# Attention on one core: waits that another wait or the queue's order covers are left out, and the planner counts two-part maxima as longer

## The chip, the cores and the metric

The kernel runs on one core of a Trainium2 chip. The metric is the device time of one execution in microseconds (us). TensorE (PE) multiplies matrices, VectorE (DVE), ScalarE (ACT) and GpSimd (POOL) work on tiles, SyncE (SP) issues most of the DMAs. Each engine works through a queue of its own, in order, and engines wait for each other on semaphores.

## The reference

One decoder block on `x` of 2048 x 1024 in float32: a norm and an input projection; eight heads of forgetting attention (FoX) and four heads of differential attention, each of them causal over 2048 positions; an output projection, a norm and a residual; and an MLP of width 4096 with squared ReLU. Only the attention matters here:

```
forgetting:    s = q k^T * scale + c_i - c_j     masked, p = softmax(s),  o = p v
differential:  s = q k^T * scale - slope * dist  for two maps of one head
               a = softmax(s0) - lam * softmax(s1),  o = rmsnorm(a v) * (1 - lam_init)
```

## The kernel before

**Tiling.** A *block* is 512 queries of one head (a FoX head has its blocks in pairs, `s` 0 and 1; a differential block has both maps). It is cut into four tiles of 128 queries, `a` = 3 to 0. A tile's keys, up to 2048, are taken in *scores* of at most 1024 keys: a tile with more than 1024 keys has two parts. All scores go through two buffers in PSUM, `ps_s`.

**Steps.** For each score: `score` (PE, products into `ps_s`), `max` (DVE, the negated maximum over the keys, L1468; for a second part also a tiny reduction over the two parts' maxima, `top`, L1472, which first waits for the reduction before it), `corr` (ACT, a second part's correction factor, L1400), `exp` (ACT, L1420, with its row sums). `fix` (POOL, L1322) scales a first part by the correction. For a differential tile, `chain` (DVE, L1489 to L1497) makes the factors from the sums, and `mix` adds the second map to the first (on POOL, or on DVE, or with `scale` on ACT). Then each block's probabilities are turned in *turns* of 128 keys: `turn` (PE, four transposes, L1581, into a ring of three PSUM tiles, `ps_t`), `hi` (ACT, L1438, a rounded copy), `lo` (DVE, L1477, the rest of it), `pv` (PE, L1596 to L1601, into `ps_o`). A block ends with `o_half` or `o_sq` (ACT, L1447, L1453), `o_add` (DVE), `rows`, `var`, `o_var`, `o_pow`, `spread` (PE, L1625), `o_scale` (DVE, L1533) and `store` (SP).

**The order.** `attention_steps` gives every step an engine, a time for which it holds the engine, a time until its result is there, what it comes after, and an urgency. `Walk.order` plays these steps through (forwards, backwards, forwards again, always the most urgent of those that are ready) and writes out one list of 3800 steps. Every engine, SP with its loads and stores among them, takes its own steps out of this one list and in its order. So on an engine the list fixes what stands before what, and a wait on that engine's result vouches for all that it did before.

**Waits.** An instruction waits for its semaphores with `wait_ge` calls ahead of it. Where there is more than one, the compiled program has, besides the wait that the instruction itself carries, an instruction EVENT_SEMAPHORE on the engine's queue ahead of it; the profile shows it under the line of the last of the calls. `hi` waits for its turn (`x_ready`, L1435) and for the `pv` that last read its buffer, four turns ago (`p_used`, L1437). `exp` waits for the turn that last read its place in `probs` (L1410), for the sums' former user (L1406, L1408), for its maximum (`maxed`, L1412), and in the second map for the `mix` two tiles back (L1248, called at L1419). `o_half` waits also on L1446, `o_sq` on L1452, `fix` on L1321, `chain` on L1487, `o_scale` on L1532.

Of the kernel before, what the change touches and what calls it, by code (L numbers as in the profile page):

```python
# [24 lines left out]
FOX, DIFF = 0, 1  # L25
# [768 lines left out]
PRING = 4  # L794
TRING = 3
SETS = 6
# [169 lines left out]
def attention_steps(blocks, scores, turns):  # L966
# [63 lines left out]
    for b in blocks:  # L1030
        ahead, mine, fox = by_block[b.n], turns_of[b.n], b.kind == FOX
        load("load_q", q_blocks[b.qb], b.n - 2, [("score", last_q[b.qb - 2])] if b.qb >= 2 else ())
        for k, sc in enumerate(ahead):
            at = b.n - 1 + SPREAD * k / len(ahead) - LEAD - (EARLY if not fox and b.J == 3 else 0)
            parts, two, keys = parts_of[b.n, sc.a, sc.s], sc.parts == 2, sc.lo + sc.width
            for p in pieces_of(sc):
                load_piece("load_k", b.u, p, b.n - 2)
            walk.step("score", sc, "PE", 0.0009 * sc.width + (0.06 if sc.part == sc.parts - 1 else 0), at + RUSH["score"],
                      [("exp", scores[sc.g - 2]) if sc.g >= 2 else None, ("load_q", q_blocks[b.qb])]
                      + [("load_k", (b.u, p)) for p in pieces_of(sc)], 0.0009 * sc.width + 0.22)  # L1040
            walk.step("max", sc, "DVE", 0.07 + 0.00104 * sc.width + (0.08 if sc.part else 0), at + RUSH["max"],
                      [("score", sc)], 0.14 + 0.00104 * sc.width + (0.14 if sc.part else 0))
            if sc.part:
                walk.step("corr", sc, "ACT", 0.19, at + RUSH["corr"], [("max", sc)], 0.29)
            after = [("max", sc)]
            if (fox or sc.s == 0) and former[b.n, sc.a] is not None:
                after.append(("turn", turns_of[former[b.n, sc.a]][-1]))
            if b.n >= SETS:
                after.append(("rows", blocks[b.n - SETS]))
            if not fox and sc.s == 1:  # L1050
                if sc.part == 0:
                    tiles.append((b.n, sc.a))
                after.append(("mix", tiles[-3]) if len(tiles) > 2 else None)
            walk.step("exp", sc, "ACT", 0.24 + 0.00084 * sc.width, at + RUSH["exp"], after, 0.34 + 0.00084 * sc.width)
            if sc.part and (fox or sc.s == 0):
                walk.step("fix", (b.n, sc.a), "POOL", 1.87, at + RUSH["fix"], [("corr", sc), ("exp", parts[0])])
            if not fox and sc.s == 1 and sc.part == sc.parts - 1:
                walk.step("chain", (b.n, sc.a), "DVE", 1.12 if two else 0.5, at + RUSH["chain"],
                          [("exp", sc), ("corr", sc) if two else None])
                if scaled(b, sc.a):  # L1060
                    walk.step("scale", (b.n, sc.a), "ACT", 0.3 + 0.00084 * keys, at + RUSH["mix"], [("chain", (b.n, sc.a))])
                    holder = "POOL", 0.15 + 0.0023 * keys
                elif on_vector(b, sc.a):
                    holder = "DVE", 1.5 if two else 0.1 + 0.0012 * keys
                else:
                    holder = "POOL", (0.8 if two else 0.4) + 0.0043 * keys
                walk.step("mix", (b.n, sc.a), *holder, at + RUSH["mix"],
                          [("scale" if scaled(b, sc.a) else "chain", (b.n, sc.a)), ("fix", (b.n, sc.a)) if two else None])
# [91 lines left out]
def attend(nc, ctx, keep, qk, vals, q_rows, k_rows, mixT, w_out, x):  # L1160
# [3 lines left out]
    turns = attention_turns(blocks)  # L1164
    opening = opening_tiles(scores)
    steps = [step for step in attention_steps(blocks, scores, turns) if step[1] not in opening]
    places, former = probability_columns(blocks)
    pairs = [[b for b in blocks if b.qb == q] for q in range(blocks[-1].qb + 1)]
    fetches, last_pair = fetched(blocks, scores)
# [5 lines left out]
    for what, arg in steps:  # L1175
        if what in ("turn", "var", "spread"):
            ring_at[what, arg] = ring
            ring += 1
    last_turn = {t.b: t for t in turns}
    last_score = {sc.b: sc for sc in scores}  # L1180
    top_no = {sc.g: n for n, sc in enumerate(sc for sc in scores if sc.part == 1)}
    fix_no = {at: n + 1 for n, at in enumerate((sc.b, sc.a) for sc in scores
# [3 lines left out]
    for sc in scores:  # L1186
        if blocks[sc.b].kind == DIFF and sc.s == 1 and sc.part == sc.parts - 1:
# [6 lines left out]
            chain_done[sc.b, sc.a] = chains  # L1194
            mix_done[sc.b, sc.a] = mixes[on_dve]
    tile_of = {n: at for at, n in tile_no.items()}

    def k_value(u, p, fox, diff):

# [47 lines left out]
    def wait_mixed(eng, b, a):  # L1247
        eng.wait_ge(mixed_dve if on_vector(blocks[b], a) else mixed, mix_done[b, a])  # L1248
# [58 lines left out]
    def gpsimd(pool):  # L1307
# [7 lines left out]
        for what, arg in steps:  # L1315
            if what == "fix":
                n, a = arg
                low = probs[:, places[n, a]:places[n, a] + 1024]
                first, second = (sc for sc in scores if (sc.b, sc.a) == arg and side(sc) == 0)
                pool.wait_ge(corrected, top_no[second.g] + 1)  # L1320
                pool.wait_ge(exped, first.g + 1)  # L1321
                pool.tensor_tensor(low, low, corr[:, n % SETS, a, 0:1].to_broadcast([P, 1024]), ALU.mult)\  # L1322
                    .then_inc(fixed, 1)
            elif what == "mix" and scaled(blocks[arg[0]], arg[1]):
# [69 lines left out]
    def scalar(act, then):  # L1394
        first_hi = next(arg for what, arg in steps if what == "hi")
        for what, arg in steps:
# [5 lines left out]
            elif what == "exp":  # L1402
                sc, par, s = arg, arg.b % SETS, side(arg)
                if sc.a == 3 and sc.part == 0 and s == 0 and sc.b >= SETS:
                    if blocks[sc.b - SETS].kind == FOX:
                        act.wait_ge(summed, fox_no[sc.b - SETS] + 1)  # L1406
                    else:
                        act.wait_ge(squared, diff_no[sc.b - SETS] + 1)  # L1408
                if sc.part == 0 and s == 0 and former[sc.b, sc.a] is not None:
                    act.wait_ge(x_ready, ring_at["turn", last_turn[former[sc.b, sc.a]]] + 1)  # L1410
                if sc.part == 0:
                    act.wait_ge(maxed, sc.g + 1)  # L1412
                    bias = nmax[:, par, sc.a, s, 0:1]
                else:
                    act.wait_ge(topped, top_no[sc.g] + 1)
                    bias = top[:, par, sc.a, s:s + 1]
                out = tile(sc) if s == 0 else tile1(sc)
                if s == 1 and sc.part == 0 and tile_no[sc.b, sc.a] >= 2:
                    wait_mixed(act, *tile_of[tile_no[sc.b, sc.a] - 2])  # L1419
                act.activation(out, ps_s[:, sc.g % 2, 0:sc.width], ACT.Exp, bias=bias,  # L1420
                               accum_out=rsum[:, par, sc.a, s, sc.part:sc.part + 1]).then_inc(exped, 1)
            elif what == "scale":
                (n, a), par, low = arg, arg[0] % SETS, 1024
                keys = (4 * blocks[n].J + a + 1) * P
                one = probs1[:, tile_no[arg] % 2, :]
                act.wait_ge(chained, chain_done[arg])
                act.activation(one[:, low:keys], one[:, low:keys], ACT.Copy,
                               scale=factor[:, par, a, 0:1]).then_inc(multiplied, 1)
                act.activation(one[:, 0:low], one[:, 0:low], ACT.Copy,
                               scale=factor[:, par, a, 1:2]).then_inc(multiplied, 1)  # L1430
            elif what == "hi":
                t, at = arg, ring_at["turn", arg]
                if t is first_hi:
                    wait_projected(act)
                act.wait_ge(x_ready, at + 1)  # L1435
                if t.n >= PRING:
                    act.wait_ge(p_used, t.n - PRING + 1)  # L1437
                act.activation(p_hi[:, t.n % PRING, t.off:512], ps_t[:, at % TRING, t.off:512], ACT.Copy)\  # L1438
                   .then_inc(hi_ready, 1)
                if t is last_turned:  # L1440
                    then()
            elif what == "o_half":
                f = fox_no[arg.n]
                act.wait_ge(p_used, last_turn[arg.n].n + 1)
                if arg.n:
                    act.wait_ge(o_free, arg.n)  # L1446
                act.activation(o_half[:, :], ps_o[64:P, :], ACT.Copy).then_inc(o_half_ready, 1)  # L1447
            elif what == "o_sq":
                d = diff_no[arg.n]
                act.wait_ge(p_used, last_turn[arg.n].n + 1)  # L1450
                if d:
                    act.wait_ge(x_ready, ring_at["var", diffs[d - 1]] + 1)  # L1452
                act.activation(o_sq[:, :], ps_o[:, :], ACT.Square).then_inc(o_squared, 1)  # L1453

    def vector(dve, then, between):
# [8 lines left out]
        for what, arg in steps:  # L1464
# [16 lines left out]
            elif what == "chain":  # L1481
                (n, a), par = arg, arg[0] % SETS
                last = max((sc for sc in scores if (sc.b, sc.a) == arg), key=lambda sc: sc.g)
                dve.wait_ge(exped, last.g + 1)
                sums = rsum[:, par, a, :, 0]
                if last.parts == 2:
                    dve.wait_ge(corrected, top_no[last.g] + 1)  # L1487
                    sums = total[:, par, a, :]
                    link(dve.tensor_scalar(sums[:, 0:1], rsum[:, par, a, 0, 0:1], corr[:, par, a, 0:1],  # L1489
                                           rsum[:, par, a, 0, 1:2], ALU.mult, ALU.add), False)  # L1490
# [36 lines left out]
            elif what == "o_scale":  # L1527
# [1 line left out]
                if q == last_spread:  # L1529
                    between()  # L1530
                dve.wait_ge(x_ready, at + 1)
                dve.wait_ge(o_free, pairs[q][-1].n + 1)  # L1532
                dve.tensor_tensor(o_sb[:, q % ORING, :], ps_t[:, at % TRING, :], o_sb[:, q % ORING, :], ALU.mult)\  # L1533
                   .then_inc(x_free, 1)
            elif what == "o_var":
# [1462 lines left out]
```

## Time and profile before

| what | value |
|---|---|
| time, median of 3 runs | 2789.02 us (2787.31 to 2791.25) |
| the profiled execution's own time | 2791.69 us |
| its span, first to last instruction | 2789.9 us |
| mean granted clock of TensorE | 0.995 |
| PE, DVE, ACT, POOL busy | 98%, 63%, 48%, 23% of the span |
| attention's own stretch | about 583 to 1370 us of the span |

The profile gives busy time by engine, by line and by stretch, the idle time of an engine ahead of an instruction with what ended it, and the chain of work that ended last. Ends of matmuls are modelled. An EVENT_SEMAPHORE is not counted as busy. `PEld` is PE's weight load, ACTq and the like are queues' own instructions.

### The profile page before, as it was taken

What the parts mean: (1) busy time and instruction counts of PE and PEld (TensorE: products, weight loads), DVE (VectorE), ACT (ScalarE), POOL (GpSimd) and SP (SyncE); (2) the same over time, 40 slices, a digit from 0 to 9 for tenths busy, and PEclk for the clock granted to TensorE, in tenths of its full rate; (3) what the DMA queues carried; (4) which work ended last, traced back from release to release, by engine and by line L of the source; (5) the groups of instructions that cost most, each with busy time, mean ns of one, the idle gap of its engine ahead of it and who ended that gap; (6) DMA issues with size and microseconds to landing.
All of it is one profiled execution on the core that took longest, in us unless ns stands there. A gap on an engine that the chain in (4) does not pass through costs nothing.

```text
span 2789.9 us, 36811 instructions
## 1 busy us (share of the span) xinstructions
PE 2726.0 (98%) x13362; PEld 2258.5 (81%) x13362; DVE 1751.8 (63%) x2495; ACT 1342.1 (48%) x2413; POOL 628.2 (23%) x558
## 2 busy tenths in 40 slices
PE   8999999989999999999999999999999999999998
PEld 6888888878788887887788788888888888888887
DVE  6211111169889899899746877887777545435567
ACT  5111111158789789688523544554444333322233
POOL 5220011125746656557311100000000000000012
PEclk9999999999999999999999999999999999999999
DMA  5343333464434515423347755575445566556666
GB/s 191 121 159 106 106 135 108 136 159 101 101 88 104 126 47 131 112 62 99 106 135 234 257 205 191 179 250 191 142 140 194 181 198 207 182 161 218 208 215 240
DMA packets 287660, 434.49 MB, mean 156 GB/s; under 512 B 19648, under 2 KB 134592, under 8 KB 287488
## 3 DMA queue, kind: packets, MB, share of 16 engines
q1 hardware_dynamic: 241664, 368.41, 42.5%
q10 hardware_dynamic: 45056, 63.05, 6.3%
q8 instruction: 101, 1.65, 0.2%
q0 software_dynamic: 768, 0.79, 0.1%
q14 instruction: 71, 0.58, 0.1%
HBM read 280.27 MB, written 151.91 MB: 155 GB/s over the span
## 4 chain that ended last, share of the span: by engine, by line
PE 85%; DVE 6%; issue 4%; ACT 2%; DMA 1%; POOL 0%; SPq 0%; POOLq 0%; ACTq 0%; DVEq 0%
PE ml_ps L2940 7%; PE ml_ps L2939 7%; PE ml_ps L2938 7%; PE ml_ps L2908 7%; PE ml_ps L2911 7%; PE ml_ps L2910 7%; PE at_ps_t L1581 5%; PE at_ps_s L1152 4%; PE pj_acc L769 4%; PE pj_acc L770 4%; PE pj_acc L771 4%; PE at_ps_s L1146 4%; DVE at_nmax L1468 2%; PE at_ps_o L1596 2%; PE at_ps_o L1597 2%
## 5 line engine op out<-in xcount | busy, mean ns | idle before, releaser
L1468 DVE TENSOR_REDUCE at_nmax<-at_ps_s 128x1 f32<-128x1024 f32 (+4 forms) x372 | 338.0, 915 | 32.6 <-PE at_ps_s L1152 30.7
L2908 PE MATMUL ml_ps<-ml_h_hiM,ml_w_hi 128*128 128x512 f32 x896 | 349.0, 389 | 1.1 <-DVE ml_t L2730 1.0
L2910 PE MATMUL ml_ps<-ml_h_loM,ml_w_hi 128*128 128x512 f32 x896 | 348.6, 389 | 0.0
L2911 PE MATMUL ml_ps<-ml_h_hiM,ml_w_lo 128*128 128x512 f32 x896 | 348.6, 389 | 0.0
L2938 PE MATMUL ml_ps<-ml_b_hi,ml_a_hi 128*128 128x512 f32 x896 | 348.5, 389 | 0.0
L2939 PE MATMUL ml_ps<-ml_b_lo,ml_a_hi 128*128 128x512 f32 x896 | 348.5, 389 | 0.0
L2940 PE MATMUL ml_ps<-ml_b_hi,ml_a_lo 128*128 128x512 f32 x896 | 348.5, 389 | 0.0
L651 DVE SCALAR_TENSOR_TENSOR pj_out_sb<-pj_acc,pj_out_sb 128x512 fp32r<-128x512 f32 x96 | 66.4, 692 | 413.6 <-ACT pj_out_sb L578 413.6
L1477 DVE TENSOR_TENSOR at_p_lo<-at_ps_t,at_p_hi 128x512 fp32r<-128x512 f32 x480 | 279.3, 604 | 33.9 <-ACT at_p_hi L1438 31.5
L1438 ACT ACTIVATE at_p_hi<-at_ps_t 128x512 fp32r<-128x512 f32 x480 | 248.0, 536 | 82.7 <-PE at_ps_t L1581 46.0
L2585 POOL TENSOR_SCALAR ml_ss<-ml_ss 128x1 f32<-128x1 f32 x16 | 17.6, 1099 | 1183.4 <-ACT ml_junk L2678 1183.1
L1581 PE MATMUL at_ps_t<-at_ident_r,at_probs 128*128 128x128 f32 x1632 | 251.8, 277 | 15.5 <-DVE at_p_lo L1477 10.2
L1420 ACT ACTIVATE at_probs<-at_ps_s,at_nmax 128x1024 f32<-128x1024 f32 (+3 forms) x244 | 230.0, 943 | 44.8 <-DVE at_nmax L1468 42.3
L578 ACT ACTIVATE pj_out_sb<-pj_acc 128x512 fp32r<-128x512 f32 x96 | 57.4, 598 | 402.6 <-PE pj_acc L771 268.9
L1581 PEld LDWEIGHTS at_ps_t<-at_ident_r,at_probs 128*128 128x128 f32 x1632 | 194.6, 142 | 58.4 <-DVE at_p_lo L1477 22.6
L1146 PE MATMUL at_ps_s<-at_k,at_q 128*128 128x512 f32 (+3 forms) x640 | 209.7, 393 | 17.8 <-ACT at_probs L1420 15.3
L1322 POOL TENSOR_TENSOR at_probs<-at_probs,at_corr 128x1024 f32<-128x1024 f32 x96 | 182.1, 1897 | 146.3 <-ACT at_corr L1400 146.0
L2365 ACT ACTIVATE ml_b_hi<-ml_b_raw 128x1024 fp32r<-128x1024 f32 x56 | 59.4, 1061 | 306.7 <-issue 159.4
L1152 PE MATMUL at_ps_s<-at_k,at_q 128*128 128x512 f32 (+3 forms) x640 | 203.1, 382 | 0.0
L2908 PEld LDWEIGHTS ml_ps<-ml_h_hiM,ml_w_hi 128*128 128x128 f32 x896 | 168.2, 188 | 36.7 <-issue 1.3
L2911 PEld LDWEIGHTS ml_ps<-ml_h_hiM,ml_w_lo 128*128 128x128 f32 x896 | 168.2, 188 | 35.0
L2939 PEld LDWEIGHTS ml_ps<-ml_b_lo,ml_a_hi 128*128 128x128 f32 x896 | 168.2, 188 | 35.0
(267 smaller groups left out, 5915.7 us busy)
## 6 DMA issues: line engine op xcount, KB each, us to landing
ml_a_raw<-ua SPq DMA_DIRECT2D x112, 512.0 KB, 3.8
qk<-pj_out_sb ACTq DMA_DIRECT2D x64, 512.0 KB, 2.8
ml_w_raw<-in_w_up_dram SPq DMA_DIRECT2D x64, 512.0 KB, 4.9
ua<-ml_t SPq DMA_DIRECT2D x128, 256.0 KB, 2.6
ml_b_raw<-in_w_down_dram SPq DMA_DIRECT2D x56, 512.0 KB, 4.8
at_q<-qk SPq DMA_DIRECT2D x96, 256.0 KB
at_k<-qk SPq DMA_DIRECT2D x96, 256.0 KB
ua<-ml_x SPq DMA_DIRECT2D x96, 256.0 KB, 2.5
```

The lines of the kernel that those rows point to most:

```text
L1146: pe.matmul(keep.ps_s[:, sc.g % 2, at:at + width], keep.q2[:, n, sc.s, q], keep.k2[:, slot, sc.s, 0:width], start=True, stop=False)
L1152: last = pe.matmul(keep.ps_s[:, sc.g % 2, at:at + width], keep.q1[:, n, sc.s, q], keep.k1[:, slot, sc.s, 0:width], start=False, stop=True)
L1438: act.activation(p_hi[:, t.n % PRING, t.off:512], ps_t[:, at % TRING, t.off:512], ACT.Copy)\
L1468: dve.tensor_reduce(nmax[:, par, sc.a, s, sc.part:sc.part + 1], ps_s[:, sc.g % 2, 0:sc.width], AX.X, ALU.max, negate=True).then_inc(maxed, 1)
L1477: dve.tensor_tensor(p_lo[:, t.n % PRING, t.off:512], ps_t[:, at % TRING, t.off:512], f32(p_hi[:, t.n % PRING, t.off:512]), ALU.subtract).t ...
L1581: last = pe.transpose(ps_t[:, at % TRING, a * P:(a + 1) * P], probs[:, key:key + P], ident)
L2908: pe.matmul(to, hi, h_hi[m][:, k, :], start=begins and k == 0, stop=False, skip_group_check=not begins)
L2910: pe.matmul(to, hi, h_lo[m][:, k, :], start=False, stop=False, skip_group_check=not begins)
L2911: last = pe.matmul(to, lo, h_hi[m][:, k, :], start=False, stop=k == 3, skip_group_check=not begins)
L2938: pe.matmul(to, hi, b_hi[b % 4][:, k, :], start=begin, stop=False)
L2939: pe.matmul(to, hi, b_lo[b % 4][:, k, :], start=False, stop=False)
L2940: last = pe.matmul(to, lo, b_hi[b % 4][:, k, :], start=False, stop=end)
```

## The change

There are two parts. In the planner the `max` of a second part holds DVE for 0.19 us more than its width asks for, where it was 0.08, and its result comes after 0.19 more, where it was 0.14. `Walk` and the urgencies stay as they are, so the list of steps may come out in another order, for all engines.

In the engines' programs a helper `precedes` tells which of two steps stands first in the list. A wait is left out where another one, or the order on the engine that is waited for, already makes sure of it: `hi` keeps one of its two waits, `exp` its maximum's and, if not vouched for, the others, `fix` and `chain` one of two, `o_half` one, `o_sq` and `o_scale` mostly one. What is computed stays the same, and so do all the instructions that compute.

```diff
-            walk.step("max", sc, "DVE", 0.07 + 0.00104 * sc.width + (0.08 if sc.part else 0), at + RUSH["max"],
-                      [("score", sc)], 0.14 + 0.00104 * sc.width + (0.14 if sc.part else 0))
+            walk.step("max", sc, "DVE", 0.07 + 0.00104 * sc.width + (0.19 if sc.part else 0), at + RUSH["max"],
+                      [("score", sc)], 0.14 + 0.00104 * sc.width + (0.19 if sc.part else 0))
...
+    place = {step: n for n, step in enumerate(steps)}
...
+    def precedes(one, other):
+        return place.get(one, -1) < place[other]
...
                 first, second = (sc for sc in scores if (sc.b, sc.a) == arg and side(sc) == 0)
-                pool.wait_ge(corrected, top_no[second.g] + 1)
-                pool.wait_ge(exped, first.g + 1)
+                if precedes(("exp", first), ("corr", second)):
+                    pool.wait_ge(corrected, top_no[second.g] + 1)
+                else:
+                    pool.wait_ge(exped, first.g + 1)
...
                 if sc.a == 3 and sc.part == 0 and s == 0 and sc.b >= SETS:
-                    if blocks[sc.b - SETS].kind == FOX:
-                        act.wait_ge(summed, fox_no[sc.b - SETS] + 1)
-                    else:
-                        act.wait_ge(squared, diff_no[sc.b - SETS] + 1)
+                    before = blocks[sc.b - SETS]
+                    if before.kind == FOX and not precedes(("spread", before.qb), ("score", sc)):
+                        act.wait_ge(summed, fox_no[before.n] + 1)
+                    if before.kind == DIFF and not precedes(("o_var", before), ("max", sc)):
+                        act.wait_ge(squared, diff_no[before.n] + 1)
                 if sc.part == 0 and s == 0 and former[sc.b, sc.a] is not None:
-                    act.wait_ge(x_ready, ring_at["turn", last_turn[former[sc.b, sc.a]]] + 1)
+                    turn = last_turn[former[sc.b, sc.a]]
+                    if not precedes(("turn", turn), ("score", sc)):
+                        act.wait_ge(x_ready, ring_at["turn", turn] + 1)
...
                 if s == 1 and sc.part == 0 and tile_no[sc.b, sc.a] >= 2:
-                    wait_mixed(act, *tile_of[tile_no[sc.b, sc.a] - 2])
+                    n, a = tile_of[tile_no[sc.b, sc.a] - 2]
+                    if not on_vector(blocks[n], a) or not precedes(("mix", (n, a)), ("max", sc)):
+                        wait_mixed(act, n, a)
...
-                act.wait_ge(x_ready, at + 1)
-                if t.n >= PRING:
+                if t.n >= PRING and precedes(("turn", t), ("pv", turns[t.n - PRING])):
                     act.wait_ge(p_used, t.n - PRING + 1)
+                else:
+                    act.wait_ge(x_ready, at + 1)
...
                 act.wait_ge(p_used, last_turn[arg.n].n + 1)
-                if arg.n:
-                    act.wait_ge(o_free, arg.n)
...
-                if d:
+                if d and not precedes(("var", diffs[d - 1]), ("pv", last_turn[arg.n])):
                     act.wait_ge(x_ready, ring_at["var", diffs[d - 1]] + 1)
...
-                dve.wait_ge(exped, last.g + 1)
                 sums = rsum[:, par, a, :, 0]
+                if last.parts == 1 or precedes(("corr", last), ("exp", last)):
+                    dve.wait_ge(exped, last.g + 1)
+                else:
+                    dve.wait_ge(corrected, top_no[last.g] + 1)
                 if last.parts == 2:
-                    dve.wait_ge(corrected, top_no[last.g] + 1)
...
-                dve.wait_ge(o_free, pairs[q][-1].n + 1)
+                follower = first_turn.get(pairs[q][-1].n + 1)
+                if follower is None or not precedes(("pv", follower), ("spread", q)):
+                    dve.wait_ge(o_free, pairs[q][-1].n + 1)
```

## Rows read from the trace of the kernel before

**Rows 1.** Busy time by stretch: us, busy (instructions) of each engine, clock, DMA.
```profile
583.00:1370.00 787.00, 753.26 (x4501) 629.25 (x4502) 707.25 (x1319) 646.59 (x1438) 457.02 (x350) 0.99 0.41 102
700.00:800.00 100.00, 94.15 (x566) 78.89 (x566) 86.52 (x176) 76.69 (x180) 60.06 (x47) 0.98 0.48 120
800.00:900.00 100.00, 97.54 (x584) 81.17 (x583) 94.17 (x162) 88.56 (x190) 57.03 (x43) 1.00 0.32 78
```

**Rows 2.** Chain that ended last in attention's stretch: by line.
```profile
by line: PE at_ps_t L1581 17.9%; PE at_ps_s L1152 13.1%; PE at_ps_s L1146 12.9%; DVE at_nmax L1468 7.5%; PE at_ps_o L1596 6.7%; PE at_ps_o L1597 6.6%; DVE at_p_lo L1477 4.9%; issue 4.7%; ACT at_probs L1420 4.0%; PE at_ps_o L1599 2.9%; PE at
```

**Rows 3.** What PE waited for in that stretch: us in total, times, longest.
```profile
PE at_ps_s L1146 <- ACT at_probs L1420: 15.3, 27, 1.0
PE at_ps_t L1581 <- DVE at_p_lo L1477: 10.2, 16, 3.4
PE at_ps_t L1608 <- DVE at_p_lo L1477: 3.5, 5, 1.1
```

**Rows 4.** What ACT, DVE and POOL waited for there, in the same columns.
```profile
ACT at_p_hi L1438 <- PE at_ps_t L1581: 46.0, 76, 2.1
ACT at_probs L1420 <- DVE at_nmax L1468: 42.3, 77, 1.5
ACT at_p_hi L1438 <- PE at_ps_o L1601: 15.7, 21, 1.4
ACT at_p_hi L1438 <- PE at_ps_o L1597: 12.1, 28, 4.2
...
DVE at_total L1489 <- ACT at_corr L1400: 2.1, 4, 0.5
...
POOL at_probs L1322 <- ACT at_corr L1400: 146.0, 74, 4.2
```

**Rows 5.** EVENT_SEMAPHORE by line: count, ns min/median/max, first and last start in us.
```profile
L1437 ACTq EVENT_SEMAPHORE  x476: 17/17/17, 589.4 to 1361.6; - x159
L1412 ACTq EVENT_SEMAPHORE  x170: 17/17/38, 622.5 to 1351.1; - x170
L1446 ACTq EVENT_SEMAPHORE  x31: 17/17/17, 595.8 to 1295.6; - x31
L1452 ACTq EVENT_SEMAPHORE  x15: 17/17/17, 751.9 to 1363.4; - x15
L1321 POOLq EVENT_SEMAPHORE  x96: 17/17/17, 599.4 to 1333.1; - x96
L1487 DVEq EVENT_SEMAPHORE  x32: 21/21/21, 691.8 to 1338.2; - x32
L1532 DVEq EVENT_SEMAPHORE  x32: 21/21/21, 599.3 to 1367.0; - x32
```

**Rows 6.** Timeline of DVE and ACT: start us, us, instruction, idle time before it.
```profile
854.51 0.95 DVE L1468 TENSOR_REDUCE at_nmax<-at_ps_s 128x1 f32<-128x768 f32 x1
...
855.49 0.15 DVE L1472 TENSOR_REDUCE at_top<-at_nmax 128x1 f32<-128x2 f32 x1
855.56 1.28 DVE L1477 TENSOR_TENSOR at_p_lo<-at_ps_t,at_p_hi 128x512 fp32r<-128x512 f32 x2
855.68 0.90 ACT L1420 ACTIVATE at_probs<-at_ps_s,at_top 128x768 f32<-128x768 f32 x1 [0.39 <-DVE at_top L1472]
...
856.57 0.97 ACT L1438 ACTIVATE at_p_hi<-at_ps_t 128x512 fp32r<-128x512 f32 x2
...
856.76 1.22 DVE L1468 TENSOR_REDUCE at_nmax<-at_ps_s 128x1 f32<-128x1024 f32 x1
...
857.42 0.30 ACT L1400 ACTIVATE at_corr<-at_nmax,at_top 128x1 f32<-128x1 f32 x1
...
857.89 0.68 DVE L1477 TENSOR_TENSOR at_p_lo<-at_ps_t,at_p_hi 128x512 fp32r<-128x512 f32 x1
...
858.07 1.12 ACT L1420 ACTIVATE at_probs<-at_ps_s,at_nmax 128x1024 f32<-128x1024 f32 x1 [0.34 <-DVE at_nmax L1468]
...
866.17 0.60 ACT L1438 ACTIVATE at_p_hi<-at_ps_t 128x512 fp32r<-128x512 f32 x1 [0.30 <-PE at_ps_o L1597]
...
866.66 1.01 ACT L1420 ACTIVATE at_probs<-at_ps_s,at_nmax 128x896 f32<-128x896 f32 x1
```

**Rows 7.** Group of the two-part maxima's second reduction in attention: busy us, mean ns.
```profile
L1472 DVE TENSOR_REDUCE at_top<-at_nmax 128x1 f32<-128x2 f32 x128 | 19.9, 155 | 4.4
```

More of the change, by code:

```diff
@@ L1178, in attend @@
             ring += 1
-    last_turn = {t.b: t for t in turns}
+    last_turn, first_turn = {t.b: t for t in turns}, {t.b: t for t in reversed(turns)}
     last_score = {sc.b: sc for sc in scores}
```

## The prediction

> **What bounds the kernel now.** I read busy time by stretch first. The change touches attention alone, 787 us of the span, and there PE is busy for 753.3 of them [rows 1], so PE idles for 33.7 us. That is all that better waits or a better order could win, since no matmul goes away. DVE is close behind with 707.3 us and ACT has 646.6. The stretches are not alike: from 800 to 900 us PE idles 2.46 us with DVE busy for 94.2, from 700 to 800 it idles 5.85 with DVE busy for 86.5 [rows 1]. Next, the chain that ended last. PE's lines lead it, but some 17% of it runs over DVE's maxima (7.5%), `lo` (4.9%) and ACT's `exp` (4.0%), with 4.7% of issue besides [rows 2]: that is where PE waits for someone. Third, whom PE waits for. Scores wait for the `exp` that frees their PSUM buffer, 15.3 us in 27 waits; turns and `var` wait for the `lo` that frees theirs, 13.7 us in 21 [rows 3]. The reader is to see that these are late answers from DVE's and ACT's queues. Whether an answer is late for its own latency or for what stands ahead of it in the queue decides what each part of the change can be worth.
>
> **Part one: the waits.** Each surplus wait is an EVENT_SEMAPHORE on its queue: 476 in front of `hi`, 170 in front of `exp`, 31 of `o_half`, 15 of `o_sq`, 96 of `fix`, 32 of `chain`, 32 of `o_scale` [rows 5]. I listed the kernel's present order and looked up both sides of each condition of the diff in it: 476 go at `hi` (309 times the turn's wait stays, 167 times the `pv`'s), 165 of 170 at `exp`, the first users' waits with them, 11 of the waits for a `mix`, all at `o_half`, `o_sq`, `fix` and `chain`, 15 of 32 at `o_scale`. That is some 840 instructions, nearly 700 of them on ACT.
>
> What is one worth? It depends on whether its engine is idle. Busy: the `exp` at 866.66 has a second wait and starts 0.11 us before the `hi` ahead of it ends (866.17 + 0.60); the `corr` at 857.42, which has one wait, starts 0.12 before the end of what is ahead of it (856.57 + 0.97) [rows 6]. So behind a busy engine the instruction costs nothing: the engine's own work hides it, and that cover goes only where the engine stands idle. Idle: the `exp` at 855.68 carries its only wait itself and starts 0.04 us after `top` ends (855.49 + 0.15); the one at 858.07 has its maximum's wait in the EVENT_SEMAPHORE and starts 0.09 after the reduction ends (856.76 + 1.22) [rows 6]. The late wait in the separate instruction costs 0.05 us.
>
> The Trainium skill's "VectorE: DVE Perf Modes", The DRAIN you can't avoid, says that a semaphore between two operations of a queue costs nothing extra; by it this whole part would be 0. The row with the busy engine agrees with it, the idle pair (0.09 against 0.04) does not.
>
> How often is the separate wait the late one? At most in all 77 waits of `exp` for a maximum, and in the 21 + 28 waits of `hi` for a `pv` [rows 4]; where a `hi` waits for its turn (76 times), that wait is the one that it carries itself, and nothing is won. So ACT's answers come earlier by at most 77 x 0.05 + 49 x 0.05 = 6.3 us in sum. PE feels that only where its own wait goes back to such an answer. The chain runs for about a quarter of its length over engines other than PE (the 17% named, issue, and smaller pieces) [rows 2], so I take a quarter: 1.6 us. The ends are 0 and 6.3. On POOL the `fix` idles for 146.0 us, always until `corr` [rows 4]; that wait stays, and the one dropped, for an `exp` that ACT did earlier, had long been met: 0. `chain` keeps the late one, 4 waits x 0.05 = 0.2, inside the 1.6. `o_half`, `o_sq` and `o_scale`: 0. No wait is added, so nothing new stands at the head of a queue.
>
> **Part two: the order.** What does a two-part maximum really hold? From the reduction's start at 854.51 to the next operation's at 855.56 are 1.05 us [rows 6]. The planner had 0.07 + 0.00104 x 768 + 0.08 = 0.95, and has 1.06 now. A one-part maximum of 1024 held 1.13 (856.76 to 857.89) [rows 6], as its formula says (1.135). So the new duration is the true one, and the plan before left out 0.11 us at each of 128 [rows 7], 14.1 us of DVE in all. In tiles with two parts DVE is nearly full (94.2 of 100), and there a plan that takes DVE for freer than it is puts `lo` and `max` later than PE needs them. That speaks for a gain. Against it: the list is made by picking the most urgent ready step with weights that stay as they are, and one longer step shifts picks on all five queues, loads and stores on SP among them, at places that have nothing to do with it; and the stretches with most idle time have DVE at 86.5, so that they lack no DVE time [rows 1]. No instruction is added or lost by this part, and every DMA is issued as before, a few steps sooner or later; PE's longest waits are for `exp` and `lo`, not for loads [rows 3].
>
> Bounds from the rows: were the whole of attention as good as 800 to 900, it would idle 787 x 2.46% = 19.4 us, 14.3 fewer; were it as bad as 700 to 800, 787 x 5.85% = 46.0, 12.3 more. Neither end is near: a reshuffle of one duration in a plan whose other durations already fit leaves most of the pattern. I take a tenth of the better end, 1.4 us of gain, because the duration is right now and nothing else is known of it.
>
> **The sum.** In the profiled execution's own time: 2791.69 - 1.6 - 1.4 = 2788.7. That execution stands 2.67 above the median of the runs, so for the median 2789.02 - 3.0 = 2786.0. What a measurement of this kernel can tell from no change is about 0.2%, 5.6 us: 2783.4 to 2794.6.
>
> **The rivals.**
>
> *The order wins several us.* PE's 15.3 and 13.7 us of waits are a lateness of DVE's and ACT's queues, and a plan with DVE's true load repairs them where it is fullest. If it takes a third of those 29.0, that is 9.7, with the 1.6 of the waits 11.3: 2777.7; with a fifth, 5.8 + 1.6: 2781.6. I put this case at 2780. For it: the 14.1 us missing from the plan. Against: the poor stretches are the ones with DVE free.
>
> *The order loses: slower than before.* The weights were fitted to a plan with the old duration. In the new plan DVE's maxima look more expensive, `lo` gets picked before `max` or the other way round at other places, and scores wait longer for `exp`. Its place is the score waits (15.3 us in 27). If they rise by 0.4 us each for twice as many, 27 x 0.4 = 10.8 less 1.6 of the waits: 2798; if by half of that, 2793, which counts as the same. It decides from an order that costs 7.2 us (5.6 + 1.6). For it: 12.3 us up to the worse stretch's level. Against: the new duration agrees with the timeline.
>
> *The waits do nothing.* Every late answer that PE feels comes from a queue that is busy ahead of it, where the dropped instruction was hidden. Then part one is 0 and the time 2789.0 - 1.4 = 2787.6, measured as no change. For it: ACT and DVE are 82% and 90% busy. Against: 77 + 49 idle waits on ACT. The rule of the skill named above gives this case, too.
>
> **How the numbers follow.** Forecast (small gain of both parts, 2786.0) 0.38; the waits do nothing and the order little 0.12; the order wins over 5.6 us 0.33; the order loses over 5.6 us in sum 0.17. So faster 0.33, same 0.50, slower 0.17. The range has to reach into both order cases: from 2776 (past the 2777.7 of a third of the waits) to 2797 (short of 2798), with about one in ten left out on either side. The forecast case's own range is 2783 to 2790, from 6.3 us of gain to none and 1 of loss.
>
> **What would show it.** The EVENT_SEMAPHOREs of L1437's, L1446's, L1452's and L1321's kind gone, those of `exp` down to a few tens, and ACT's `hi` and `exp` busy times as before. An `exp` that idles for its maximum starts 0.04 after it, not 0.09. ACT's idle time before `hi` with a `pv` as releaser falls only by a few us, as does PE's idle time of 33.7. If the order is what matters, the stretches of 100 us change by more than 1 us each, in both directions, PE's waits for `exp` and `lo` change in number, and the sum of idle DVE time moves with it. I am wrong if attention's stretch shortens by more than 8 us, or lengthens; then the term for the order was mis-sized, and which stretch it came from tells whether two-part tiles (DVE full) or one-part tiles did it. Outside attention nothing should move.

## The result, and the profile after

The changed kernel takes 2806.74 us (median of 6 runs, 2805.11 to 2809.74) against 2788.26 of the kernel before, measured beside it: 18.5 us slower, a ratio of 1.0065 (95% interval 1.0055 to 1.0075). I had forecast 2786.0, range 2776 to 2797, and had given slower 0.17.

The head of the changed kernel's page, and its two busiest engines:

```profile
span 2805.2 us, 35973 instructions
## 1 busy us (share of the span) xinstructions
PE 2726.4 (97%) x13362; PEld 2261.7 (81%) x13362; DVE 1753.5 (63%) x2495; ACT 1345.0 (48%) x2413; POOL 628.9 (22%) x558
```

No computing instruction came or went, and 838 instructions of the queues are gone (36811 before). The two profiled executions lie 15.3 us apart (spans 2789.9 and 2805.2 us), and PE is busy 2726.4 us in this one against 2726.0 before: PE idles 78.8 us against 63.9, so nearly all of the difference is idle time. Busy time by stretch, first the kernel before, then the changed one (columns as in [rows 1]):

```profile
583.00:620.00 37.00, 33.62 (x192) 27.82 (x193) 30.26 (x52) 28.45 (x66) 13.82 (x13) 0.92 0.95 214
620.00:640.00 20.00, 19.39 (x117) 15.90 (x116) 18.32 (x32) 16.75 (x39) 10.34 (x9) 1.00 0.22 54
640.00:700.00 60.00, 59.43 (x356) 49.91 (x354) 57.64 (x98) 53.98 (x110) 34.91 (x26) 1.00 0.44 103
700.00:1300.00 600.00, 575.14 (x3454) 480.72 (x3454) 543.34 (x1015) 497.29 (x1112) 351.85 (x269) 0.99 0.39 98
```

```profile
583.00:620.00 37.00, 29.79 (x167) 24.77 (x168) 25.77 (x45) 24.16 (x56) 9.81 (x10) 0.92 0.99 222
620.00:640.00 20.00, 17.71 (x102) 14.76 (x101) 15.13 (x26) 13.39 (x33) 9.95 (x9) 0.93 0.21 54
640.00:700.00 60.00, 59.28 (x355) 50.05 (x354) 56.65 (x94) 53.55 (x111) 34.26 (x29) 1.00 0.41 95
700.00:1300.00 600.00, 570.06 (x3438) 478.95 (x3439) 541.61 (x1007) 496.62 (x1105) 350.36 (x267) 0.99 0.40 98
```

In the first 57 us of attention PE does 5.5 us less work (47.50 against 53.01) and DVE 7.7 less (40.90 against 48.58), though the stage has barely begun. The kernel before makes its first ten transposes at 584.41 us and the changed one at 585.17; counted from there, 57 us hold 4.8 us less of PE (49.67 against 54.42) and 6.7 less of DVE (42.30 against 48.98). From 620 to 640 TensorE's granted clock is 0.93 against 1.00, behind 37 us in which PE was busy for 29.8 instead of 33.6. The 600 us after 700 lose 5.1 of PE. What PE waited for in attention, in the changed kernel (columns as in [rows 3]):

```profile
PE at_ps_s L1146 <- ACT at_probs L1431: 26.2, 37, 1.9
PE at_ps_t L1595 <- DVE at_p_lo L1487: 13.8, 24, 3.3
PE at_ps_t L1622 <- DVE at_p_lo L1487: 4.9, 5, 2.7
```

Against [rows 3], the scores' wait for `exp` grew from 15.3 to 26.2 us, and the wait of turns and `var` for a free place in the ring from 13.7 to 18.7. The timeline of the beginning shows why. First the kernel with the waits left out and the old order (run waits_alone below), then the changed one (start us, us, instruction, idle time before it):

```profile
583.15 2.71 PE L1595 MATMUL at_ps_t<-at_ident_r,at_probs 128*128 128x128 f32 x10 [3.25 <-DVE at_p_lo L1487]
585.51 1.10 PE L1146 MATMUL at_ps_s<-at_k,at_q 128*128 128x512 f32 x2
...
587.84 0.57 PE L1146 MATMUL at_ps_s<-at_k,at_q 128*128 128x512 f32 x2
```

```profile
585.17 2.71 PE L1595 MATMUL at_ps_t<-at_ident_r,at_probs 128*128 128x128 f32 x10 [3.35 <-DVE at_p_lo L1487]
587.53 0.78 PE L1610 MATMUL at_ps_o<-at_p_hi,at_v_sb 128*128 128x512 f32 x1
...
593.73 0.70 PE L1146 MATMUL at_ps_s<-at_k,at_q 128*128 128x512 f32 x2
...
610.20 0.73 PE L1146 MATMUL at_ps_s<-at_k,at_q 128*128 128x512 f32 x2 [1.64 <-ACT at_probs L1431]
...
618.62 0.75 PE L1146 MATMUL at_ps_s<-at_k,at_q 128*128 128x512 f32 x2 [1.91 <-ACT at_probs L1431]
...
623.92 0.73 PE L1146 MATMUL at_ps_s<-at_k,at_q 128*128 128x512 f32 x2 [0.72 <-ACT at_probs L1431]
...
627.93 0.74 PE L1146 MATMUL at_ps_s<-at_k,at_q 128*128 128x512 f32 x2 [1.20 <-ACT at_probs L1431]
```

The old order issues the first score 2.4 us after the first turn, the new one 8.6 us after it, behind turns and `pv` that were ready. Those are then used up: from 610 on PE stands four times in front of a score, 5.5 us in all, while the next blocks' scores go one by one through `score`, `max` and `exp`. With the old order there is one such wait between 600 and 645, of 0.33 us. The lists of steps say the same: score 12 stands behind 7 turns in the old and 11 in the new, score 16 behind 10 and 16; and in blocks 4 and 5 the new list has the two parts of all eight tiles back to back on PE, the old one of one.

### The profile page after: what moved, and what is told of

Read it like the earlier page. It is cut to its first block, busy times and chain, and to the rows that moved or that the text cites. A ratio compares the mean times of both kernels' runs of the same rounds, so it can differ in the third digit from the quotient of the medians.

```text
span 2805.2 us, 35973 instructions
## 1 busy us (share of the span) xinstructions
PE 2726.4 (97%) x13362; PEld 2261.7 (81%) x13362; DVE 1753.5 (63%) x2495; ACT 1345.0 (48%) x2413; POOL 628.9 (22%) x558
## 4 chain that ended last, share of the span: by engine, by line
PE 85%; DVE 6%; ACT 4%; issue 4%; DMA 1%; POOL 0%; SPq 0%; POOLq 0%; ACTq 0%; DVEq 0%
PE ml_ps L2954 7%; PE ml_ps L2953 7%; PE ml_ps L2952 7%; PE ml_ps L2922 7%; PE ml_ps L2925 7%; PE ml_ps L2924 7%; PE at_ps_t L1595 5%; PE at_ps_s L1152 4%; PE at_ps_s L1146 4%; PE pj_acc L769 4%; PE pj_acc L771 4%; PE pj_acc L770 4%; DVE at_nmax L1478 2%; ACT at_probs L1431 2%; PE mo_acc L1910 2%
## 5 line engine op out<-in xcount | busy, mean ns | idle before, releaser
L1146 PE MATMUL at_ps_s<-at_k,at_q 128*128 128x512 f32 (+3 forms) x640 | 211.2, 395 | 29.1 <-ACT at_probs L1431 26.2
```

The costliest lines, as they stand in the source:

```text
L1146: pe.matmul(keep.ps_s[:, sc.g % 2, at:at + width], keep.q2[:, n, sc.s, q], keep.k2[:, slot, sc.s, 0:width], start=True, stop=False)
```

## The experiments

Each kernel leaves attention's computation whole. Times are medians; "slower" and "faster" are differences to the kernel before, measured beside each group: 2788.84 us for experiments 1 to 4, 2789.05 for 5, 6, 9 and 10, 2788.57 for 7 and 8, and 2788.87 for 11 to 14. "Above the waits alone" adds the 3.5 us of experiment 1 to that difference. Each kernel ran 10 or 11 times, but order_alone, h12 and hold_only 4 times and refit 5. The old and the new list are the step lists that the planner makes with the old and with the new duration of a two-part maximum. Unless said otherwise a kernel has the waits left out. Code is cut to the lines that matter.

**1. waits_alone**: the changed kernel with the old durations. Against the changed kernel:

```diff
-            walk.step("max", sc, "DVE", 0.07 + 0.00104 * sc.width + (0.19 if sc.part else 0), at + RUSH["max"],
-                      [("score", sc)], 0.14 + 0.00104 * sc.width + (0.19 if sc.part else 0))
+            walk.step("max", sc, "DVE", 0.07 + 0.00104 * sc.width + (0.08 if sc.part else 0), at + RUSH["max"],
+                      [("score", sc)], 0.14 + 0.00104 * sc.width + (0.14 if sc.part else 0))
```

> The waits are left out, the planner's durations stay at 0.08 and 0.14, so the list of steps is that of before. If the order alone makes the changed kernel 18.5 us slower: 2783 to 2789, some 1.6 us faster than before, at most 6.3. If the missing waits are the cause (a wait that now stands inside an instruction blocks something that the separate one did not): near 2800 or above. If the missing waits do nothing: 2788, within 1 us of before.

2785.3 us, 3.5 faster than before, ratio 0.9984 (0.9975 to 0.9993). Leaving the waits out helps, by twice the 1.6 I had put on it (the interval allows 2.0 to 7.0 us). The pair of lines that shows one of them, DVE and ACT of this kernel:

```profile
854.20 1.21 DVE L1478 TENSOR_REDUCE at_nmax<-at_ps_s 128x1 f32<-128x1024 f32 x1
```

```profile
855.45 1.11 ACT L1431 ACTIVATE at_probs<-at_ps_s,at_nmax 128x1024 f32<-128x1024 f32 x1 [0.29 <-DVE at_nmax L1478]
```

It is the same `exp` as the one at 858.07 of [rows 6]. It starts 0.04 us after the reduction ends (854.20 + 1.21), not 0.09, and ACT stood idle 0.29 us before it, not 0.34. The whole trace agrees. Of the 77 `exp` that waited for a maximum before, 49 started 0.08 to 0.12 us after it, 9 at 0.03 or 0.04, and in the other 19 something else ended the wait (0.37 us or more); now 50 start at 0.03 or 0.04 and none at 0.08 to 0.12. A `hi` that waited for a `pv` started 0.09 or 0.10 after it in 49 of 50 cases, and now at 0.03 to 0.05 in all 51. PE's own idle time fell from 63.9 to 61.1 us over the two executions.

**2. order_alone**: the two new numbers in the kernel before, its waits untouched.

> The new durations in the kernel before, with all its waits. If the order is the cause and the waits give 1.6 us: 2807 to 2810, PE's waits for exp near 26 us as in the changed kernel against 15.3 before. If the waits are the cause: 2788 within 3. If the two work only together: in between.

2809.78, 20.9 slower, ratio 1.0069 (1.0053 to 1.0084), and PE waits 26.8 us for `exp`. The order is the whole loss. Waits and order add up: 20.9 - 3.5 = 17.4, where both together measured 18.5.

**3. and 4. new_start, old_start**: one list up to turn 96, the other behind it. Turn 96 is not the last of the first head's, as the text below has it: it lies in block 9, the second block of the first differential head. For new_start (old_start has the two pairs of durations the other way round):

```diff
+    one, two = ([step for step in attention_steps(blocks, scores, turns, long) if step[1] not in opening]
+                for long in ((0.19, 0.19), (0.08, 0.14)))
+    one = one[:one.index(("turn", turns[96])) + 1]
+    steps = one + [step for step in two if step not in set(one)]
```

> The list of the changed kernel up to turn 96 (the last of the first head's), the list of before behind it; waits left out. The times at which blocks end show 9.8 us lost by the end of the first head, where the new list does 11 and 16 turns ahead of scores 12 and 16 instead of 7 and 10. If the loss is one at the start: 2796 to 2800. If it is a loss in every head (DVE's order inside two-part tiles) that only shows early: under 2793. If the loss at the start is given back later when the old order follows: 2788.

> The list of before up to turn 96, that of the changed kernel behind it; waits left out. If the start has 9.8 of the loss and the last differential head most of the rest (about 4): 2792 to 2798. If the start had nothing to do with it: 2803 or more.

2797.22 (8.4 slower, ratio 1.0027, 1.0018 to 1.0036) and 2795.43 (6.6 slower, 1.0021, 1.0011 to 1.0030). Measured from the waits alone, the new start costs 11.9 and the rest 10.1, together the 22.0 that lie between waits_alone and the changed kernel. So the part up to turn 96 is half of it, and nothing gives it back. Where blocks end says where the rest goes. Count, ns, then the first and last start in us of `o_half` (its last is block 43) and `o_sq` (block 8 first, block 47 last), for waits_alone, old_start and new_start:

```profile
L1457 ACT ACTIVATE at_o_half<-at_ps_o x32: 593/595/600, 589.8 to 1291.3; 64x512 f32<-64x512 f32 x32
L1463 ACT ACTIVATE at_o_sq<-at_ps_o x16: 597/598/617, 720.0 to 1359.5; 128x512 f32<-128x512 f32 x16
```

```profile
L1460 ACT ACTIVATE at_o_half<-at_ps_o x32: 594/595/598, 591.3 to 1297.6; 64x512 f32<-64x512 f32 x32
L1466 ACT ACTIVATE at_o_sq<-at_ps_o x16: 588/598/613, 721.5 to 1371.7; 128x512 f32<-128x512 f32 x16
```

```profile
L1460 ACT ACTIVATE at_o_half<-at_ps_o x32: 594/595/598, 589.0 to 1302.7; 64x512 f32<-64x512 f32 x32
L1466 ACT ACTIVATE at_o_sq<-at_ps_o x16: 597/600/614, 729.6 to 1370.9; 128x512 f32<-128x512 f32 x16
```

With the new start the delay is there at block 8 (729.6 against 720.0, of which 1.3 us stood ahead of attention's first ten transposes, 584.46 against 583.15) and grows by 1.8 more (11.4 at the end). With the old start it is 1.5 at block 8, which began as much later (591.3 against 589.8), 6.3 at block 43 and 12.2 at block 47: the heads between cost about 5, the last differential head 6 more. These are single executions, and old_start's is 2.0 us above its median, so the parts are known to a us or two.

**5. and 6. new_to_15, new_15_to_96**: the new list in a part of the start only, the old one elsewhere. For new_to_15 (the other kernel has old, new, old in place of new, old, old):

```diff
+    for part, turn in ((new, 15), (old, 96), (old, len(turns))):
+        part = part[:part.index(("turn", turns[turn])) + 1] if turn < len(turns) else part
+        steps += [step for step in part if step not in set(steps)]
```

> The changed kernel's list up to turn 15 alone, then the list of before; waits left out. In that short stretch scores 12 to 15 come 4 to 6 turns late and scores 16 to 20 stand behind all 16 turns. Theory A, the first scores are late and DVE and ACT lose time at once that they, nearly full, never get back: most of the 11.9 us that the new start costs, 2793 to 2797. Theory B, it is the pairing behind it (both parts of each tile of blocks 4 and 5 back to back on PE and on DVE, 8 pairs against 1): 2786 to 2789.

> The list of before up to turn 15, that of the changed kernel from there to turn 96, then that of before; waits left out. Theory A (late first scores): 2785 to 2788. Theory B (pairs back to back in blocks 4 and 5): 2793 to 2797. Both: each of these two kernels 2789 to 2792.

2790.84 (ratio 1.0006, 0.9996 to 1.0016) and 2793.8 (1.0013, 1.0003 to 1.0022): 5.3 and 8.3 us above the waits alone. Neither theory has it to itself, and the second kernel is 1.8 above what I had expected if both hold. Sixteen turns' worth of steps in the new order, at the very beginning, cost 5.3 us by themselves; of DVE's busy time in the first 37 us 4.4 are missing (26.88 against 31.30), and the old order behind does not win them back. First waits_alone, then new_to_15:

```profile
583.00:620.00 37.00, 34.92 (x203) 28.93 (x204) 31.30 (x55) 28.33 (x68) 13.43 (x13) 0.95 0.88 204
```

```profile
583.00:620.00 37.00, 31.49 (x171) 25.42 (x172) 26.88 (x47) 24.61 (x58) 10.58 (x11) 0.92 0.91 205
700.00:1300.00 600.00, 576.78 (x3474) 482.51 (x3473) 545.75 (x1023) 501.63 (x1119) 355.54 (x271) 1.00 0.39 98
```

**7. paired**: in the list of before the two parts' steps of blocks 4 and 5 are put back to back, nothing else.

```diff
+    for one, two in zip(scores, scores[1:]):
+        if one.b in (4, 5) and one.part == 0 and two.part == 1:
+            for what in ("score", "max", "exp"):
+                steps.remove((what, one))
+                steps.insert(steps.index((what, two)), (what, one))
```

> The list of before with one thing altered: in blocks 4 and 5 the score, max and exp of a tile's first part are moved to right before those of its second part (8 tiles), as the changed kernel's list has them back to back; waits left out. If the pairing is what costs in turns 15 to 96 (that stretch cost 7.0 us): 2790 to 2794. If it is that the scores as a whole come behind more turns: 2785 to 2787.

2788.78, ratio 0.9999 (0.9989 to 1.0009): 3.7 above the waits alone, between the two expectations. The pairing costs, but is under half of the 8.3 of its stretch. What is left goes with the scores standing behind more turns; that part was not tried apart from it.

**8. new_end**: the old list up to turn 440, the new one behind it.

> The list of before up to turn 440, that of the changed kernel behind it (the last two two-part differential blocks), waits left out. The times at which blocks end in the kernel with the old start put 4.7 us of its loss behind block 44. If a late place of the last scores costs by itself: 2789 to 2792, with nothing behind it that could give it back. If the loss there was carried over from the heads before: 2785 to 2787.

2791.07, ratio 1.0009 (0.9999 to 1.0018), 6.0 above the waits alone. The end costs by itself. There the new list puts scores 364 and 365, of block 46, behind turns 448 to 450, where the old one has them ahead of those. It moves other steps there too, so that it is these two that cost is not shown.

**9. h12**: hold 0.12, result 0.14.

> The hold of a two-part maximum 0.12, its result 0.14; waits left out. The list then starts as before (scores 12 and 16 behind turns 7 and 10), though the planner gives it a later planned end (778.8) than to the changed kernel's list (775.4; before 767.1). If the start's order decides: 2786 to 2793. If the planned end tells the time: over 2808. If any list other than the one the weights were fitted to is worse by about the same: 2795 or more.

2804.91, 15.9 slower (1.0050, 1.0033 to 1.0067). I was wrong here: the good start did not save it. Its PE order is that of before up to turn 20. Its `o_half` and `o_sq` rows put most of the loss behind block 8:

```profile
L1457 ACT ACTIVATE at_o_half<-at_ps_o x32: 594/595/597, 591.3 to 1313.7; 64x512 f32<-64x512 f32 x32
L1463 ACT ACTIVATE at_o_sq<-at_ps_o x16: 592/597/610, 728.0 to 1383.2; 128x512 f32<-128x512 f32 x16
```

8.0 later than waits_alone at block 8 (the first `o_half` was 1.5 later already), 22.4 at block 43, 23.7 at block 47; this execution, 2808.89 us, is 4.0 above its median. So the start is not what decides in general; a list can lose in any head.

**10. hold_only**: hold 0.14, result 0.19. This is not the pair that the text below describes: the kernel that ran has the two numbers the other way round. Against the changed kernel:

```diff
-            walk.step("max", sc, "DVE", 0.07 + 0.00104 * sc.width + (0.19 if sc.part else 0), at + RUSH["max"],
+            walk.step("max", sc, "DVE", 0.07 + 0.00104 * sc.width + (0.14 if sc.part else 0), at + RUSH["max"],
                       [("score", sc)], 0.14 + 0.00104 * sc.width + (0.19 if sc.part else 0))
```

> The hold 0.19, the result still 0.14; waits left out. Its list starts as the changed kernel's does (11 and 16 turns ahead of scores 12 and 16, 8 pairs in blocks 4 and 5), the later heads as before in their pairs. If the start costs 11.9 wherever it stands: 2796 or more. If the result time is what spoils the list: 2788 or less.

2808.14, 19.1 slower (1.0062, 1.0045 to 1.0079). Its list starts as the changed kernel's does (11 and 16 turns ahead of scores 12 and 16, eight pairs in blocks 4 and 5), and it is as bad. Whether the hold or the result spoils a list it does not tell, since both are above their old values; a hold of 0.19 with a result of 0.14 was not run. That a longer hold is enough to lose is shown by h12, whose result is the old one.

**11. corr21**: the maxima's durations as before, but `corr` held for 0.21 instead of 0.19.

> The old durations of maxima and the waits left out, but a duration that has nothing to do with maxima, corr on ACT, taken as 0.21 for 0.19 (the planned end 766.4 against 767.1). It displaces 308 of PE's 1380 steps, 6 of them by more than 3 places; the changed kernel displaces 613 and 52. If any new list costs (the old one is fitted): 2790 to 2800. If the loss comes from what is displaced far, above all the first scores and the last block's: 2784 to 2788.

2787.76, 1.1 faster than before (0.9997, 0.9987 to 1.0006), 2.4 above the waits alone. A new list need not cost 15 us; this one displaces few steps by more than three places (6 of PE's, the changed kernel 52) and keeps the start. But the count does not rank the lists: h12 displaces 23 so far and refit 109, and they lost 15.9 and 14.5 us.

**12. refit**: the new durations, with weights searched for the least planned end.

```diff
-RUSH = {"score": -1.113, "max": -0.06, "corr": 0.71, "exp": 0.362, "fix": 0.648, "chain": -1.388,
-        "mix": 0.875, "turn": 0.08, "hi": 0.131, "lo": -0.136, "pv": 0.259}
-SPREAD, LEAD, EARLY = 1.186, 0.433, 1.624
+RUSH = {"score": -1.123, "max": -0.106, "corr": 0.562, "exp": 0.306, "fix": 0.704, "chain": -1.489,
+        "mix": 0.875, "turn": 0.076, "hi": 0.108, "lo": 0.282, "pv": 0.259}
+SPREAD, LEAD, EARLY = 1.186, 0.429, 1.624
```

> The changed kernel (durations 0.19, waits left out) with other weights: RUSH and LEAD searched for 60 seconds off the chip for the least planned end under the new durations, 766.7 against the 775.4 of the changed kernel; played with the new durations the list of before ends at 770.1. If the new duration is good and only the weights no longer fitted it, and the planned end tells the order of lists: below 2785, faster than the waits alone. If the planned end does not tell what the chip does, and the weights of before had been picked by measured times: 2793 or more, with twice as many steps displaced as in the changed kernel.

2803.33, 14.5 slower (1.0040, 1.0026 to 1.0053). The planned end fell by 8.7 and the chip gave back 4. For the planner's own clock the refit is better than the list of before played with the same durations (766.7 against 770.1), on the chip it is 18 us worse than that list without the waits.

**13. and 14. hi_waits_kept, exp_waits_kept**: as waits_alone, but `hi` or `exp` keeps its surplus waits.

> The list of before, all waits left out but those of hi: its 476 stay. The waits in all are worth 3.5 us. If it is exp's answer after a maximum (0.05 us each, on the way score, max, exp, next score) that is felt: 2785 to 2786, as without hi's. If it is hi's: 2788.

> The list of before, all waits left out but those of exp (its former turn, the sums' former user, the mix). If exp's are the ones that are felt: 2788 to 2789. If hi's are: 2785 to 2786. If both: each of these two kernels 2786 to 2787.

2787.43 (0.9993, 0.9984 to 1.0002) and 2786.94 (0.9992, 0.9983 to 1.0001). Either kept group takes back about half of the 3.5 us, which fits both being felt; but the intervals overlap each other and that of waits_alone, so the division is not shown. The traces show that each group acts where it should: with `hi`'s waits kept, 52 of its 53 starts behind a `pv` are again at 0.09 or 0.10 us and 46 `exp` at 0.03 or 0.04; with `exp`'s kept, 47 `exp` are at 0.08 to 0.12.

## Why the prediction was wrong, point by point

- **What bounds attention**: right. PE waits for late answers of ACT and DVE, for scores above all. The score waits, 15.3 us before and 26.2 after, took 10.9 of the 14.9 us by which PE idles more, as the rival of a losing order named.
- **The waits, 1.6 us (0 to 6.3)**: right in kind and in sign, and inside the ends; the term was half of what it measured, 3.5. The separate wait costs about 0.06 us where ACT is idle (0.10 against 0.04 after the `pv` or the maximum). It was the late one in 49 of the 77 waits for a maximum, not in all, and in 49 for a `pv`: 98 x 0.06 = 5.9 us of earlier answers, an estimate near the 6.3. So it was the quarter, taken from the chain's shares, that was too small: 2.8 us less idle time on PE and 3.5 us of the median are about half of those 5.9, though the interval's lower end, 2.0, is a third. The chain's shares do not say how much PE gains from an earlier answer. The waits-do-nothing rival is out. What the prediction sets against this from the Trainium skill's "VectorE: DVE Perf Modes", The DRAIN you can't avoid, was measured with a semaphore behind each of eight VectorE copies in a row; it does not speak of a second wait ahead of an idle ScalarE, so it gave no 0 for this part.
- **The count of instructions**: 838 gone, some 840 forecast.
- **The duration**: right as a measurement, in the one tile read (1.05 us held, 1.06 planned). It did not carry over into a better list.
- **The order, 1.4 us of gain**: this step failed. The term measured 20.9 us of loss. I reasoned "the duration is right now", so the list should gain, and bounded a loss by the worse stretch's idle share, 12.3 us. Both were unfounded. The list comes from a greedy pass that takes the most urgent ready step by weights that fitted the old numbers; a truer number makes the pass choose differently, not better. The planner's own clock says so: with the new duration, the list of before ends at 770.1 and the list that the planner makes ends at 775.4. I had not asked what the old list is worth under the new numbers. And the bound took the worst 100 us between 700 and 800 as the worst that an order can do, while the new order made a worse one at the start (PE idles 9.5 us of 57, where it idled 4.0 before).
- **The rival of a losing order**: its mechanism was right, and its rise of the score waits too (10.8 us, measured 10.9), though by luck: its words have the waits twice as many and 0.4 us longer, its sum takes 27 of them, and they were 37 (longest 1.9, where it was 1.0). Its time (2798) was 9 short, since it left the ring's waits where they were (5.0 more) and counted nothing else. Its chance of 0.17 was too low. I held against it that the duration agreed with the timeline, which was no argument.
- **What in the order costs** is shown in part: half up to turn 96, where the first scores come 6 us late and 16 turns of new order cost 5.3 us; 6 in the last differential head, where among other moves two scores stand behind three turns; pairing of two parts 3.7. At the start the trace shows how: the scores' chain over DVE and ACT (90% and 82% busy in attention) begins late, and PE later has nothing else to do. For the end this is argued from the list. What costs the 5 us in the heads between, and in h12's later heads, was not taken apart. That the old weights were chosen by times on the chip would explain why every larger reordering (changed, h12, hold_only, refit) lost 14 to 19 us; the runs agree with that and do not show it.

The version that beats both kernels is waits_alone: 2785.3 us, the waits left out and the old numbers kept.

## What to carry to other kernels

Where an order is written by a planner, an edit to one of its durations is an edit to the whole order. That the number got truer says nothing of the new list. Play the old list with the new numbers first: a new list that is worse than that by the planner's own clock is suspect before it runs. Passing proves nothing: refit had the best planned end under its durations, and lost 14.5 us. Nor do a list's ends tell: h12's first and last scores stand where they did, and it lost 15.9. Only the run tells. A surplus wait was hidden behind a busy ACT here and cost about 0.06 us where it was the late one, so count idle waits alone. And ship such two edits apart: here 3.5 us of gain were hidden under 21 of loss.

## What the runs showed of the hardware

With one list a delay can come through whole. Behind block 8 the kernel new_to_15, which follows the order of waits_alone from turn 15 on, is 5.4 us later at its first `o_sq` (725.4 against 720.0), 5.5 at the last `o_half` (1296.8 against 1291.3) and 5.6 at the last `o_sq` (1365.1 against 1359.5):

```profile
L1462 ACT ACTIVATE at_o_half<-at_ps_o x32: 594/595/598, 588.2 to 1296.8; 64x512 f32<-64x512 f32 x32
L1468 ACT ACTIVATE at_o_sq<-at_ps_o x16: 597/600/617, 725.4 to 1365.1; 128x512 f32<-128x512 f32 x16
```

In this pair 640 us of attention on five engines keep an early delay to within 0.2 us.

It is not so in every pair. new_end has the order of waits_alone up to turn 440. It comes to block 8's `o_sq` 1.8 us later (721.8 against 720.0) and to block 9's only 0.4 later, and the distance is then still 0.7 at the last `o_half` (1292.0 against 1291.3). Between the two, TensorE's granted clock fell in waits_alone and not in new_end; PE had been busy 18.3 us of the 20 before in both, so why it fell is not known. First waits_alone, then new_end, each with the ten us of the drop and block 9's `o_sq`:

```profile
720.00:730.00 10.00, 8.95 (x44) 7.50 (x45) 8.34 (x19) 6.81 (x17) 8.97 (x6) 0.83 0.11 25
752.14 0.60 ACT L1463 ACTIVATE at_o_sq<-at_ps_o 128x512 f32<-128x512 f32 x1 [1.51 <-PE at_ps_o L1615]
```

```profile
720.00:730.00 10.00, 8.57 (x53) 7.04 (x52) 9.02 (x21) 7.57 (x20) 8.97 (x7) 1.00 0.27 67
752.54 0.60 ACT L1468 ACTIVATE at_o_sq<-at_ps_o 128x512 f32<-128x512 f32 x1 [1.52 <-PE at_ps_o L1620]
```

So some 1.4 us of position between two executions of the same steps go with one drop of the clock, and a loss read from one pair of traces can be off by as much.

The clock also takes a share of what a list costs. The same 13362 matmuls keep PE busy for 2722.5 us in waits_alone (granted clock 0.996), 2726.4 in the changed kernel (0.994), 2728.7 in h12 (0.993), 2731.3 in hold_only and 2733.0 in refit (both 0.992). Of the 20.6 us between the spans of waits_alone and refit, 10.5 are busy time and 10.1 idle time. PE idled more in the slower kernels and was granted less clock, in refit 0.74 from 1160 to 1180 us; how much of each kernel's loss the clock adds was not tried apart.
